# Joining the second half's projections to the output-and-state block, pairing its state outputs, and splitting the latent scores

## The reference

```python
x = layer_norm(x, ln_emb_g, ln_emb_b)
z = x @ w_in
xs, gs, cq, ckv, kr, gm = jnp.split(z, IN_SPLIT_POINTS, axis=-1)   # 512, 512, 256, 128, 64, 512 columns
y = gelu(s5_states(xs) + d_skip * xs)
ys = y * sigmoid(y @ w_glu + b_glu) * silu(gs)
q = rms_norm(cq) @ w_uq        # 4 heads of 128 plain + 64 rotary columns
kv = rms_norm(ckv) @ w_ukv     # 4 heads of 128 key + 128 value columns
s = (q_nope @ k_nope.T + rotary(q_rope) @ rotary(kr).T) * 192 ** -0.5   # causal, per head
ym = softmax(s) @ v * silu(gm)
mix = concatenate([ys, ym]) @ w_out
u = ALPHA * x + mix
out = layer_norm(u + sigmoid(u @ w_pg) * (p @ w_pp))
```

## Time and profile before

| | us |
|---|---|
| median of the three runs (lowest, highest) | 2261.66 (2257.03, 2278.43) |
| the profiled execution | 2257.28 |
| its span | 2255.0 |
| PE busy in the span | 2113.6 (94%) |
| DVE busy | 1060.8 (47%) |
| ACT busy | 639.4 (28%) |
| POOL busy | 246.5 (11%) |

### The profile page before, as it was taken

How to read it: one execution, slowest core, us unless ns; L and a number is a source line. 1 busy time by engine, 2 the same in 40 slices (tenths; PEclk the granted TensorE clock), 3 DMA queues, 4 the chain that set the end, 5 groups by cost and what they waited for, 6 DMA issues and landing times. The chain is left out here.

```text
span 2255.0 us, 23160 instructions
## 1 busy us (share of the span) xinstructions
PE 2113.6 (94%) x9419; PEld 1534.2 (68%) x9419; DVE 1060.8 (47%) x1721; ACT 639.4 (28%) x1047; POOL 246.5 (11%) x131
## 2 busy tenths in 40 slices
PE   5886999999999999999999999999998989989997
PEld 1453547588777777777777887777666655559875
DVE  5685879953032322322322216899732323451345
ACT  4523212122223233333333321012223533240232
POOL 0110002112211111111111211000002100000000
PEclk9998999999999999999999999999999999999999
DMA  7311022301301111111112215221101120020100
GB/s 261 126 56 56 19 70 80 103 19 47 112 29 39 38 39 39 38 39 38 38 29 94 66 29 179 82 76 51 22 26 40 28 107 1 1 117 34 56 38 37
DMA packets 127121, 135.23 MB, mean 60 GB/s; under 512 B 14603, under 2 KB 106194, under 8 KB 125977
## 3 DMA queue, kind: packets, MB, share of 16 engines
q1 hardware_dynamic: 121723, 111.58, 15.5%
q0 software_dynamic: 5152, 22.15, 2.6%
q10 hardware_dynamic: 142, 0.03, 0.0%
HBM read 116.77 MB, written 15.80 MB: 59 GB/s over the span
## 5 line engine op out<-in xcount | busy, mean ns | idle before, releaser
L172 PE MATMUL banks<-h_hi,fr_w_rest 128*128 128x512 f32 x1152 | 465.7, 404 | 10.5 <-DVE h_rest L907 5.4
L173 PE MATMUL banks<-h_rest,fr_w_hi 128*128 128x512 f32 x1152 | 450.4, 391 | 0.0
L174 PE MATMUL banks<-h_hi,fr_w_hi 128*128 128x512 f32 x1152 | 449.9, 391 | 0.0
L172 PEld LDWEIGHTS banks<-h_hi,fr_w_rest 128*128 128x128 f32 x1152 | 216.7, 188 | 85.8 <-issue 35.4
L174 PEld LDWEIGHTS banks<-h_hi,fr_w_hi 128*128 128x128 f32 x1152 | 216.7, 188 | 47.3
L173 PEld LDWEIGHTS banks<-h_rest,fr_w_hi 128*128 128x128 f32 x1152 | 217.1, 188 | 41.9 <-issue 1.0
L1497 DVE COPY arena<-banks 128x768 f32<-128x768 f32 (+1 forms) x64 | 52.8, 825 | 371.9 <-PE banks L1258 371.9
L1178 POOL TENSOR_TENSOR fr_w_rest<-arena,fr_w_hi 128x1024 fp32r<-128x1024 f32 x45 | 107.5, 2389 | 529.9 <-ACT fr_w_hi L1341 529.9
L490 PE MATMUL banks<-arena 128*128 128x512 f32 x256 | 120.3, 624 | 35.7 <-issue 31.5
L1364 ACT ACTIVATE arena<-banks,arena 128x512 f32<-128x512 f32 x92 | 63.2, 687 | 259.8 <-PE banks L174 259.7
L766 DVE SCALAR_TENSOR_TENSOR arena<-arena 128x1024 f32<-128x1024 f32 (+5 forms) x108 | 129.0, 1195 | 3.7
(11 more groups left out here) (348 smaller groups left out, 3421.4 us busy)
## 6 DMA issues: line engine op xcount, KB each, us to landing
arena<-in_w_in SPq DMA_DIRECT2D x80, 512.0 KB, 3.8
arena<-in_w_ada POOLq DMA_DIRECT2D x6, 2048.0 KB, 18.8
arena<-in_x SPq DMA_DIRECT2D x4, 1024.0 KB, 18.9
arena<-in_fwd SPq DMA_DIRECT2D x16, 256.0 KB, 5.0
filter_spectra<-arena POOLq DMA_DIRECT2D x2, 2048.0 KB, 6.6
arena<-in_inv SPq DMA_DIRECT2D x16, 256.0 KB, 2.6
arena<-filter_spectra SPq DMA_DIRECT2D x2, 2048.0 KB, 8.4
arena<-in_w_out SPq DMA_DIRECT2D x8, 512.0 KB, 8.3
```

Source lines behind the costliest of these rows:

```text
L172: nc.tensor.matmul(out, ll, rh, start=start, stop=False)
L173: nc.tensor.matmul(out, lh, rl, start=False, stop=False)
L174: return nc.tensor.matmul(out, lh, rh, start=False, stop=stop)
```

## The change

Three parts; the diff is cut to what the text speaks of.

`project_second(K, gelu_done, y_ready, lat_ready)` no longer opens a block: it returns functions for each engine, which `output_and_states` calls inside its own block, and its barrier is gone. POOL, SP, PE, ACT and DVE go on from the one into the other. The rounding and splitting of the columns of `x2T` move up between the latents, the first weight tile is loaded early, projections 0 and 1 run ahead of the transposes of the gelu result. There are three places for weight tiles (`w_at`: tile 0 in the first, odd tiles in the second, even ones in the third). `w_uq` and `w_ukv` are loaded during the projections.

`outputs(q)` makes both halves g2 of four indices and alternates between them.

In `latent_attention` queries and keys are kept as fp32r parts, two heads at a time. The two halves of the 128 rows of `kr_parts` hold the rounded rotary key and its remainder; the rounded rotary query stands in both halves, its remainder in the lower half, with zeros in the upper one. The scores are five fp32r products over 128 rows, each at least 256 columns wide. The up-projections of a head are six jobs ("x": two each for the plain queries, the keys and the rotary queries) in the order of the transpose jobs; those of head 0 come ahead of the units, those of head h + 1 in the steps of the first six units of head h. Each ends with an ACT rounding and a DVE subtraction. Values are still projected for all heads at once.

```diff
@@ output_and_states
+        second = project_second(K, gelu_done, y_ready, lat_ready)
@@ POOL, SP
             nc.gpsimd.memset(K.at(S5M, 4096), 0.0).then_inc(m_clear, 1)
+            second.remainders(pool)
...
+            second.loads(sp)
@@ PE
-                half = slice(64 * g2, 64 * g2 + 64)
                 for i in range(4):
                     j = 4 * q + i
-                    out = PS[:, y_bank[n], i * P:(i + 1) * P]
-                    nc.tensor.matmul(out, U[:, g2, j, :], M[:, g2, j, :], start=True, stop=False)
-                    nc.tensor.matmul(out, G[0][half, j, :], QR[half, j, 1:9, :], start=False, stop=False)
-                    last = nc.tensor.matmul(out, G[1][half, j, :], QN[half, j, 1:9, :], start=False, stop=True)
+                    for g2 in range(2):
+                        nc.tensor.matmul(out(g2, i), U[:, g2, j, :], M[:, g2, j, :], start=True, stop=False)
+                    for state, taps in ((G[0], QR), (G[1], QN)):
+                        for g2 in range(2):
+                            half = slice(64 * g2, 64 * g2 + 64)
+                            last = nc.tensor.matmul(out(g2, i), state[half, j, :], taps[half, j, 1:9, :], start=False, stop=(taps is QN))
...
-            for i in range(3):
+            for i in range(4):
                 latents(i)
             pe.wait_ge(toeplitz, 16 * TC)
-            for n in range(8):
-                outputs(n)
-                if n < 5:
-                    latents(3 + n)
+            for q in range(4):
+                outputs(q)
+                if q < 2:
+                    latents(4 + 2 * q)
+                    latents(5 + 2 * q)
+            second.products(pe)
@@ ACT
                 nc.scalar.copy(lat[:, i, :], PS[:, i % 2, 0:448]).then_inc(lat_ready, 1)
+                if i == 0:
+                    act.wait_ge(v_mm, 8)
+                if i < 4:
+                    second.round_columns(i)
+                if i == 4:
+                    second.round_columns(7)
+            for k in range(4, 7):
+                second.round_columns(k)
+            act.wait_ge(h_ready, 4)
+            second.round_weights(act, 0)
...
+            second.evictions(act)
@@ DVE
             for n in range(8):
                 q, g2 = n // 2, n % 2
+                if n == 4:
+                    dve.wait_ge(lat_mm, NT)
+                    for k in range(KT):
+                        second.rest_of_columns(dve, k)
                 dve.wait_ge(y_mm, n + 1)
...
+            second.vectors(dve)
@@ project_second, as functions
+        tile(0)
...
+        sp.wait_ge(gelu_done, 4)
+        tile(1)
+        sp.dma_start(wglu, io["w_glu_2"][0].rearrange("(k p) n -> p k n", p=P)).then_inc(glu_in, 16)
+        tile(2)
...
+        pe.wait_ge(y_ready, 4)
+        project(0)
+        project(1)
+        pe.wait_ge(gelu_done, 4)
+        pe.wait_ge(lat_ready, NT)
+        for n in range(8):
...
+            if n >= 6:
+                pe.wait_ge(y_taken, n - 5)
...
+        project(2)
+        pe.wait_ge(pos_ready, 1)
+        pe.wait_ge(y_taken, 8)
+        nc.tensor.transpose(PS[:, 7, 0:NT], posf[0:NT, :], ident[0:NT, 0:NT]).then_inc(pos_tr, 1)
+        for n in range(3, 8):
+            project(n)
...
+    def evictions(act):
+        round_weights(act, 1)
...
+        take_projection(0)
+        take_projection(1)
+        for n in range(8):
...
+            nc.scalar.copy(dst, PS[:, y_tr_bank[n], :].rearrange("p (a b) -> p a b", b=P)).then_inc(y_taken, 1)
+        for n in range(2, 8):
+            take_projection(n)
...
+        for h in range(2):
+            dve.wait_ge(l_taken, 7 + h)
+            rows = kr_parts[64:128, h * 512:(h + 1) * 512]
+            link(nc.vector.tensor_tensor(rows, PS[64:128, 2 + h, :], rows.bitcast(fp32), ALU.subtract))
@@ latent_attention, scores on PE
-                    e = min(n, c + 512)
+                    e = max(min(n, c + 512), c + 256)
                     out = PS[:, 2 * (u % 2) + c // 512, 0:e - c]
-                    nc.tensor.matmul(out, qnT[:, h, i * P:(i + 1) * P], knT[:, h, c:e], start=True, stop=False)
-                    last = nc.tensor.matmul(out, qrT[half, h // 2, i * P:(i + 1) * P], krT[half, c:e], start=False, stop=True)
+                    nc.tensor.matmul(out, nl[:, rows], kh[:, c:e], start=True, stop=False)
+                    nc.tensor.matmul(out, nh[:, rows], kl[:, c:e], start=False, stop=False)
+                    nc.tensor.matmul(out, rl[:, rows], kr_parts[:, c:e], start=False, stop=False)
+                    nc.tensor.matmul(out, rh[:, rows], kr_parts[:, c:e], start=False, stop=False)
+                    last = nc.tensor.matmul(out, nh[:, rows], kh[:, c:e], start=False, stop=True)
...
+            def project_up(g):
+                _, h, n, _ = t_jobs[g]
+                if g >= 2:
+                    pe.wait_ge(t_taken, g - 1)
+                out, cols = PS[:, 4 + g % 2, :], slice(n % 2 * 512, n % 2 * 512 + 512)
+                if n < 2:
+                    for c in range(2):
+                        last = nc.tensor.matmul(out, wuq[:, c, h, 0:128], cqT[:, c, cols], start=(c == 0), stop=(c == 1))
+                elif n < 4:
+                    last = nc.tensor.matmul(out, wuk[:, h, :], ckvT[:, cols], start=True, stop=True)
+                else:
+                    for i in range(4):
+                        row = rope_rows[h // 2][:, 4 * (n % 2) + i, h % 2, :]
+                        for half in (slice(0, 64), slice(64, 128)):
+                            last = nc.tensor.matmul(PS[half, 4 + g % 2, i * P:(i + 1) * P], row, ident, start=True, stop=True)
+                last.then_inc(t_done, 1)
...
+            pe.wait_ge(r_ready, NT)
+            pe.wait_ge(v_ready, NT)
+            for g in range(UPS):
+                project_up(g)
@@ at the end of each step, on PE, ACT and DVE
+                if next_up(step) is not None:
+                    project_up(next_up(step))
...
+                    round_up(next_up(step))
...
+                    rest_of_up(next_up(step))
@@ the rotation on DVE
-                    ins = nc.vector.tensor_tensor(rope_rows[:, i, :, out:out + 32], t1, t2, op)
+                    for pair in range(2):
+                        ins = nc.vector.tensor_tensor(rope_rows[pair][:, i, :, out:out + 32], t1[:, 2 * pair:2 * pair + 2, :], t2[:, 2 * pair:2 * pair + 2, :], op)
```

More of the change, by code:

```diff
@@ L10 @@
 from contextlib import ExitStack
+from dataclasses import dataclass
+from typing import Callable
 import numpy as np
@@ L2079, with project_second @@
 RMS_EPS = 1e-6
-def project_second(K):
+W_UQ, W_UK, W_UV = SECW + 7248, LATS + 400, LATW + 3072
+@dataclass
+class SecondProjection:
+    loads: Callable
+    remainders: Callable
+    products: Callable
+    round_columns: Callable
+    round_weights: Callable
+    evictions: Callable
+    rest_of_columns: Callable
+    vectors: Callable
+def project_second(K, gelu_done, y_ready, lat_ready):
     nc, io, PS = K.nc, K.io, K.PS
     ident, cols2, x2T = K.at(IDENT, P), K.at(COLS2, 64), K.at(X2T, KT, S)
-    cqT, ckvT, krT = K.at(CQT, 2, S), K.at(CKVT, S), K.at(KRT, S)
+    cqT, ckvT, kr_parts = K.at(CQT, 2, S), K.at(CKVT, S), K.part("key_rope", KRT, S)
+    K.kr_parts = kr_parts
     lat = K.at(LAT, NT, 448)
@@ L2099, in project_second @@
     red, t1, t2 = K.at(YG + 1792, NT, 32), K.at(YG + 2048, NT, 32), K.at(YG + 2304, NT, 32)
-    w_slots, wglu = K.at(SECW, 2, KT * P), K.at(SECW + 2 * KT * P, 4, CH)
-    o = SECW + 2 * KT * P + 4 * CH
-    w_parts = [(K.part(f"p2_w{j}_hi", o + j * KT * P, KT * P), K.part(f"p2_w{j}_rest", SECW + j * KT * P, KT * P)) for j in range(2)]
-    o += 2 * KT * P
-    assert LATW + 3 * S <= LAT and YG + 2560 + S <= YGT
-    places = [LATW, LATW + S, LATW + 2 * S, YMT, YMT + S, YMT + 2 * S, o, YG + 2560]
+    COLUMN7 = SECW + 6 * S
@@ new lines, in project_second @@
+    w_places = [(YST + S, COLUMN7 + S)] + [(SECW + (2 + n) * S, SECW + n * S) for n in range(2)]
+    w_raw = [K.at(raw, KT * P) for _, raw in w_places]
+    w_split = [(K.part(f"p2_w{n}_hi", hi, KT * P), K.part(f"p2_w{n}_rest", raw, KT * P)) for n, (hi, raw) in enumerate(w_places)]
+    w_at = lambda T: 0 if T == 0 else 2 - T % 2
+    wglu = K.at(SECW + 4 * S, 4, CH)
+    places = [S5W + k * S for k in range(4)] + [LATW + k * S for k in range(3)] + [COLUMN7]
+    assert COLUMN7 == S5B and COLUMN7 + 2 * S <= S5B + 2080 and S5TMP == YST and LATW + 3 * S <= LAT
@@ L2276 @@
+    return SecondProjection(loads, remainders, products, round_columns, round_weights, evictions, rest_of_columns, vectors)
 MLA_HEADS, ROPE_D = 4, 64
@@ L2350, in _ @@
-            pe.wait_ge(r_ready, NT)
-            for n in range(4):
-                pair, h = n // 2, n % 2
-                for i in range(4):
-                    last = nc.tensor.transpose(PS[:, 4 + n, i * P:(i + 1) * P], rope_rows[:, 4 * h + i, 2 * pair:2 * pair + 2, :], ident)
-                last.then_inc(rt, 1)
-            pe.wait_ge(up_ready, 24)
-            pe.wait_ge(rt_ready, 4)
```

(4 more changed lines are left out.)

425 lines of the change are left out of this document (220 added, 205 removed).

## The result

The changed kernel takes 2198.82 us (median of four runs, 2198.21 to 2206.47); the kernel before, run beside it, 2259.78. The ratio is 0.972, with a 95% interval of 0.966 to 0.978. The forecast was 2208 with a range of 2194 to 2230.

The account below looks back on a forecast made before the run. PE's order was taken to set the end everywhere. Gains of 13.5 + 14.7 + 5.5 + 13.5 + 3.8 = 51.0 us off 2257.3 gave 2206.3, taken as 2208 for a median; range 2194 to 2230 for 8 in 10.

Parts of the forecast that it names:

- 1, outputs: Latents and state outputs: paired outputs cost 1.28 us an index, 20.4 us for 16, a gain of 13.5 us.
- the pairs do not overlap: State outputs: 64-row products in different halves do not run together; gain there 3.3 us, total 2218; chance 0.10.
- 2, join: Last output to end of projection 7: 66.8 us become 52.1, gain 14.7, bounds 5 and 19.3.
- 3 us of waiting: After the 24 transposes of the gelu result: PE waits 3 us for the first two copies.
- 1.6: Projections after PE's wait at the transposes: 1.6 us taken for a start at half clock, up to 3 possible.
- the join gives nothing but the barrier: Outputs to projections: PE waits behind gelu as long as before; gain there 5 us, total 2218; chance 0.10.
- 3, between: Between projections and attention: the 8.54 us wait for `w_ukv` falls to 3, gain 5.5 us, ends 0 and 7.
- 4, ahead of the units: Stretch before the attention units: 41.7 us become 28.2 (rotations to 19.1, six jobs 9.1), gain 13.5 us.
- 5, units: Attention units: scores gain 28.0 us, up-projections inside cost 22.2, waits 2; gain 3.8 us, from -12 to 8.
- Narrow fp32r products laid bare by their weight loads: Scores in the units: a 0.11 us weight load exposed in every product, 26 us in all, total 2234; chance 0.08.
- Units as a round trip: Units: 18 steps with a job each uncovered by 3.6 us, 65 us in all, total 2272; chance 0.04.
- The signs: Units: wrong if eighth unit's scores exceed 2.7 us, PE idles beyond 10 us, or the clock falls.

Follow-up runs that it names:

- the control: The changed kernel run once more with no edit; median 2200.68 us over four runs, ratio 0.976 (0.974 to 0.977) to the kernel before.

## Why the prediction was right, and where not

**1, outputs.** Right in the sum, and in part wrong in its split. 1.28 an index was forecast, 1.285 measured. The 0.42 as a product and a switch holds. The prediction gave 10.2 us to the overlap and 3.3 to the fewer switches; measured are 7.0 and 6.2. It had priced 64-row products without overlap at 0.32 each, and four in a row take 1.09. Since the price with overlap was read from the earlier trace rows by itself, this did not reach the sum, but the rival "the pairs do not overlap" would have come out 3 us lower than its 2218. Nor does the picture hold that the overlap comes from products in different halves standing next to each other. Both orders tried, in turn and two by two, overlap alike.

**2, join.** Right in mechanism; the terms "3 us of waiting" and "1.6" for the clock were mis-sized. They measured 0.56 and nothing. Projections 0 and 1 over gelu (11.0 for 10.9) and 24 transposes (2.78) came as written, ACT's wait for the tile was 3.99 for 4. But the copies had begun at 1688.09, before PE's last free transpose, so that only 0.28 was left twice. Behind these two waits the clock stayed at 1.00. Where PE did wait here, the clock cost more than the 1.6 taken: 2.8 us behind the 5.64 of the run with gelu first, 3.1 behind the 2.98 of the one with the subtractions late. The rival "the join gives nothing but the barrier" is refuted.

**3, between.** PE waited 3.8 us where 3 had been taken.

**4, ahead of the units.** 28.9 us for 28.2. The rotations took 1803.92 to 1821.05, 17.1 us for 17.0 forecast; two half-size instructions are 0.36 us together. The six jobs took 10.1 (1821.25 to 1831.35) for 9.1: PE waited 0.49 and 0.38 inside them and 1.40 behind them.

**5, units.** Here the prediction was off by 5.1 us, and all of it the right way. The scores gained 31.5 us, not 28.0. The term that was too dear is 0.11 us for going into fp32r and again for coming out, 1.8 a head. PE's timeline at the last eighth unit of the changed kernel:

```profile
1947.73 1.28 PE L2506 MATMUL banks<-arena 128*128 128x128 f32 x10
1948.77 0.48 PE L2454 MATMUL banks<-ml_kn_hi,ml_qn_rest 128*128 128x512 f32 x1
1949.08 0.40 PE L2455 MATMUL banks<-ml_kn_rest,ml_qn_hi 128*128 128x512 f32 x1
```

From the first fp32r product to the second it is 0.31 us instead of 0.227, but the first begins early: ten float32 records at 0.112 would reach 1948.85, and the second fp32r product starts 0.23 behind that. So neither way shows a cost here, and the 0.34 of the earlier trace rows, which stands behind 64-row products, need not be the price of this change of type. A head without up-projections inside went from 33.35 us (1964.08 to 1997.43, between two eighth units) to 25.09 (1923.68 to 1948.77), 8.3 less where 7.0 were computed.

The up-projections with their waits cost 160.2 - 137.7 + 3.4 = 25.9 for 24.2, by the run with float32 scores. And 3.4 us were never in the sum. Windows of the kernel before at the start of its units:

```profile
1872.70:1875.00 2.30, 2.27 (x8) 1.27 (x8) 0.46 (x3) 0.49 (x2) 0.00 (x0) 0.85 0.02 7
1875.00:1880.00 5.00, 5.00 (x11) 2.36 (x11) 1.98 (x10) 1.25 (x5) 0.00 (x0) 0.50 0.01 2
1880.00:1882.00 2.00, 2.00 (x4) 0.29 (x2) 0.00 (x0) 0.31 (x2) 0.00 (x0) 0.71 0.00 0
```

0.15 x 2.3 + 0.50 x 5 + 0.29 x 2 = 3.4 us were lost to the clock. The earlier trace rows had it in plain sight as a mean of 0.98 for the stretch; I took the head from a later, undisturbed period and left the first units out. 31.5 - 25.9 + 3.4 = 9.0 is the measured gain again; it is no check, since the 25.9 was itself worked out from these stretches. In an execution like the control's, half of the 3.4 is lost again.

**The rivals.** Narrow fp32r products laid bare by their weight loads: the 256-column products stand 0.12 apart, in line with 0.227 for 512, so refuted at the widths the kernel uses. At 128 columns a product takes 0.11 and not 0.06, as it would if a load were laid bare; no run shows that the load is what bounds it. Units as a round trip: not so, but the margin was narrower than "some 4 us a step lie over it": it decided from 2.8 us uncovered, and of 0.7 us more in each round trip nearly two thirds already came through.

**The signs.** Of what would have shown it wrong, the eighth unit's scores stayed under 2.7 us (2.4) and PE's idle time in the units under 10 (6.1). The third, a clock that falls in the units, did not come in the first trace but did in the control and three others, at 1.7 us each; it did not undo the gain. Two of the numbers to look for did not follow from the prediction's own terms. The first scores "near 1851" should have read 1825.5 (1872.7 less 13.5, 14.7, 5.5 and 13.5); they came at 1831.35, with the 7.6 us of the late start in it. A head of units "near 33.5" is 34.4 by the terms (33.36 - 7.0 + 7.4 + 0.7), and 34.4 and 34.0 were measured.

The misses of the parts add up to 6.9 us: 3.5 and 5.1 from parts 2 and 5, -0.2, -0.8 and -0.7 from parts 1, 3 and 4. Another 1.7 had been added for the median, which makes 8.6 of the 9.2 us to the measured one. That the profiled execution (2206.47) stands on the sum (2206.3) is luck: the 6.9 us gained beyond the forecast met a part ahead of the change that ran 7.6 us longer.

## What to carry to other kernels

A wait taken from PE can be worth more than its length, by the half clock behind it: 5.6 us of wait cost 8.4 here, and 3.0 cost 6.1. The extra does not follow from the wait's length alone, since 2.2 us cost none at another place and 1.4 cost none or 1.7 at a third. So when a stretch is priced, read its granted clock in pieces of a few us, the first ones above all, and not as a mean. And a round trip PE, ACT, DVE, PE that shows no wait may still be near its limit; doubling one link of it is a cheap way to see the slack.

## What had not been expected of the hardware

**Order of issue in two halves.** Products in different halves overlapped whether they were issued in turn or two by two, 0.65 us for four either way; in one half 1.09. In the traces the products of the two halves start within 0.02 us of each other. The Trainium skill, "TensorEngine Tiling (Array Packing)", section "Key Properties", calls the tiles independent, and these runs agree.

**The clock with two outcomes at one place.** The first 4 us of the units had 1.00 in the first trace and 0.56 and 0.59 in the control, behind the same 1.4 us of waiting. Ahead of it the mean clock was 0.94 in the one and 0.89 in the other. What decides was not tried.

**DVE held by POOL.** DVE's and POOL's timeline in the changed kernel:

```profile
1668.57 2.35 DVE L2290 TENSOR_TENSOR p_x_rest<-arena,p_x_hi 128x1024 fp32r<-128x1024 f32 x2
1670.85 3.39 DVE L2290 TENSOR_TENSOR p_x_rest<-arena,p_x_hi 128x1024 fp32r<-128x1024 f32 x1
...
1670.18 2.97 POOL L2185 TENSOR_TENSOR p_w_rest<-arena,p_w_hi 128x1024 fp32r<-128x1024 f32 x1 [78.35 <-ACT p_w_hi L2243]
```

Of eight like subtractions seven take 1.2 us and the one that starts inside POOL's takes 3.39; POOL's ends at 1673.15. The same happened before the change, twice (2.43 and 3.38 us, beside POOL's 2.35 and 2.81), and makes up the 12.55 us of the earlier trace rows against the 9.17 of eight that run alone. There the second of them kept PE waiting 2.34 us in projection 0; now PE is still at the outputs when it happens. The Trainium skill, "SBUF — State Buffer", section "SBUF: two separate sides", says that the port pair DVE and GpSimd share is an exclusive lock, which the one that starts first holds for its whole instruction while the other waits. The trace agrees: the subtraction ends at 1674.24, 1.1 us behind POOL's, and took 2.2 us more than its neighbours.
